# A fused transformer layer on one core: first modulation parts and first input chunks regrouped by K

## The chip, the cores and the metric

The kernel runs on one core of one Trainium2 chip. The metric is the device time of one execution in microseconds; lower is better. The times are medians of three runs.

## The reference

One encoder layer in float32 for a sequence of 256 rows and a width of 2048. A vector c gives shift, scale and gate (six vectors of 2048, `mod = silu(c) @ w_mod + b_mod`), and everything after it hangs on the first two of them:

```python
mod = silu(c) @ w_mod + b_mod                    # 2048 -> 6 * 2048
sh1, sc1, gt1, sh2, sc2, gt2 = split(mod, 6)
h = x * (1.0 + sc1) + sh1                        # (256, 2048)
proj = h @ w_in                                  # 2048 -> 5828 columns
p_a, p_b, p_c, p_d = split(proj, (A_COLS, B_COLS, C_COLS, D_COLS))
y = concat(rwkv7(p_a), sparse_attention(p_b), chunk_attention(p_c), retention(p_d))
x = layer_norm(ALPHA * x + (1 + gt1) * (y @ w_out))
h = x * (1.0 + sc2) + sh2
gate, up = split(h @ w_up, (D_FF, D_FF))
x = layer_norm(ALPHA * x + (1 + gt2) * ((silu(conv(gate)) * up) @ w_down))
```

The columns A of the input projection belong to RWKV: r, k and v of 512 columns each, and 256 "lora" columns. Group B holds the queries of the sparse attention and, among others, 256 indexer columns (QI).

## The kernel before

**The input pass.** The product with w_in runs over 12 blocks of output columns, each over 16 K tiles of 128 rows. Its unit is the chunk: two K tiles by 512 columns (512 KB), 96 chunks in all (`N0_OUT`, 8 a block, `CH_IN`). Float32 is made of two parts: ScalarE copies a chunk from RAW to WHI as fp32r (`split_hi`), VectorE writes the rest to WLO (`split_lo`), and TensorE sums three products a tile (`fm`, 24 matmuls a chunk). h is split in the same way, to HHI and HLO. RAW, WHI and WLO are rings of four chunks; SP issues the load of chunk n once the low part of chunk n - 4 is done, and splits run 3 chunks ahead of TensorE (`AHEAD`).

**The order of the chunks.** `chunk_at(n)` gives block and K pair. Blocks 0 (r) and 1 (k) are interleaved: chunks 0 to 3 and 4 to 7 are the first eight K tiles of blocks 0 and 1, chunks 8 to 15 the other eight. From chunk 16 on it is block after block: 2 is v, 3 is lora and QI together, 4 and 5 are B, 6 to 8 C, 9 to 11 D. Each block has two of the four PSUM banks G (`pair`).

**The modulation.** w_mod is read by POOL as tiles of 128 partitions by 1024 columns (512 KB, one row of 4 KB a partition) into the four buffers of MODR; 16 tiles make a part of 1024 columns, and 12 parts make the whole. VectorE adds each tile, times a column of silu(c), to ACC (`mod_add`, L781 for the first tile of a part, L784 for the others; `mod_done` counts them and frees the buffer). TensorE sums over the partitions (`mod_reduce`, 8 matmuls with one column), and VectorE adds the bias (`mod_cols`, L791). The first four parts are shift and scale, in the order `FIRST_PARTS`: first half of the shift, first half of the scale, then the second halves. After the first two, h for K tiles 0 to 7 can be made (`dve.tensor_scalar` at L829, ScalarE L505, `h_split` L816), and chunks 0 to 7 run (`FIRST_CHUNKS`); after the other two, h for K tiles 8 to 15.

**Order by hand.** Every engine has its instruction order written out. After the first chunks the engines walk through n and its two halves: in each they have a chunk half, a number of mod tiles (`mods_at`), and a step of other work: `SETUP` (RWKV's preparation: squares, norms, four reciprocals "inverse", lora, cumulate, hats), the RWKV stages (`RW`, 21 stages for each of 4 units, from chunk `RW_FROM` = 35 on), and from `AT_FROM` = 79 on the attention and retention steps (`MIX`). When a block is done (`DONE_IN`), ScalarE and VectorE evacuate it (`evac_in`); for RWKV's columns these are 14 tiles of PA (L513, L852). VectorE executes in order, so a wait in an evacuation also holds the next low part behind it.

## Time and profile before

| | us |
|---|---|
| median of 3 runs | 1523.93 (1523.52 to 1525.11) |
| profiled execution, span | 1521.2 |
| TensorE busy (PE) | 1358.8 |
| VectorE busy (DVE) | 1025.9 |
| ScalarE busy (ACT) | 558.0 |
| TensorE's waits for VectorE's ACC | 73.6 |

A row of the timeline has start and duration in us, engine, source line, operation, the tiles written and read with their shapes, the count, and in square brackets the idle time before it with what ended it. A line of the table by windows has the window, its length, busy time of each engine with its number of instructions, the granted clock of TensorE (1.00 is 2.4 GHz, 0.50 is 1.2 GHz), the mean busy share of the 16 DMA engines and GB/s. The line number L1347 is the helper of all matmuls, so the tiles tell them apart.

### The profile page before, as it was taken

How to read it: one execution, taken by the hardware profiler on the slowest of the kernel's cores; microseconds unless marked ns; L12 is line 12 of the kernel's file. 1: busy time of each engine (PE TensorE's matmuls, PEld its weight loads, DVE VectorE, ACT ScalarE, POOL GpSimd, SP SyncE). 2: the span in 40 equal slices, each digit the busy share in tenths (PEclk: the TensorE clock that was granted, in tenths of full speed). 3: DMA queues.
4: the chain of work that ended last, by engine and by line, in shares of the span. 5: the costliest groups of instructions: out<-in, count | busy, mean ns of one | idle time of the engine just before them, and what ended most of it. 6: DMA issues, size and time to landing. Idle time of an engine off the chain costs nothing.

```text
span 1521.2 us, 23831 instructions
## 1 busy us (share of the span) xinstructions
PE 1358.8 (89%) x9247; PEld 1252.2 (82%) x9247; DVE 1025.9 (67%) x1320; ACT 558.0 (37%) x771; POOL 137.3 (9%) x221
## 2 busy tenths in 40 slices
PE   1172998999999999998699999999999999999994
PEld 1172998998979667786699999999999998888883
DVE  4787778768787986566977877655556555545545
ACT  2021553213233342443344444444444444333331
POOL 2222010100000110100600000000000000000001
PEclk8585999889999998999899999999999999999997
DMA  9898884645555764665178786554655656766561
GB/s 354 314 338 309 268 276 130 200 144 180 194 167 167 277 233 141 246 226 178 55 280 288 251 289 196 162 181 147 199 183 175 193 179 193 244 199 193 181 205 57
DMA packets 142951, 319.08 MB, mean 210 GB/s; under 512 B 12238, under 2 KB 19744, under 8 KB 141856
## 3 DMA queue, kind: packets, MB, share of 16 engines
q1 hardware_dynamic: 114656, 213.23, 43.1%
q0 software_dynamic: 28224, 104.87, 20.2%
q8 instruction: 48, 0.79, 0.2%
q14 instruction: 23, 0.19, 0.0%
HBM read 315.97 MB, written 2.10 MB: 209 GB/s over the span
## 4 chain that ended last, share of the span: by engine, by line
PE 47%; DVE 2%; issue 1%; DMA 1%; ACT 0%; DVEq 0%; ACTq 0%; SPq 0%
PE G L1347 46%; DMA RAW<-in_w_up_dram 1%; PE M L1347 0%; DVE WLO L770 0%; DVE X L1331 0%; DVE X L1340 0%; DVE X L1338 0%; DVE SM L1259 0%; ACT WHI L487 0%; DVE ACC L1250 0%; DVE GF L1266 0%; DVE HLO L816 0%; DVE X L1314 0%; DVE SM L1316 0%; DVE SM L1255 0%
## 5 line engine op out<-in xcount | busy, mean ns | idle before, releaser
L1347 PE MATMUL G<-HHI,WHI 128*128 128x256 f32 x1952 | 566.1, 290 | 19.3 <-issue 7.2
L1347 PE MATMUL G<-HLO,WHI 128*128 128x256 f32 x1952 | 557.5, 286 | 0.0
L1347 PE MATMUL G<-HHI,WLO 128*128 128x256 f32 x1952 | 557.3, 286 | 0.0
L1347 PEld LDWEIGHTS G<-HHI,WHI 128*128 128x128 f32 x1952 | 379.8, 195 | 23.4 <-issue 20.0
L1347 PEld LDWEIGHTS G<-HLO,WHI 128*128 128x128 f32 x1952 | 380.1, 195 | 0.5 <-issue 0.5
L1347 PEld LDWEIGHTS G<-HHI,WLO 128*128 128x128 f32 x1952 | 379.8, 195 | 0.0
L765 DVE TENSOR_TENSOR WLO<-RAW,WHI 128x1024 fp32r<-128x1024 f32 x210 | 256.2, 1226 | 175.1 <-ACT WHI L481 172.9
L481 ACT ACTIVATE WHI<-RAW 128x1024 fp32r<-128x1024 f32 x210 | 221.5, 1060 | 316.0 <-PE G L1347 274.9
L770 DVE TENSOR_TENSOR WLO<-RAW,WHI 128x1024 fp32r<-128x1024 f32 x174 | 210.5, 1228 | 153.7 <-ACT WHI L487 153.7
L487 ACT ACTIVATE WHI<-RAW 128x1024 fp32r<-128x1024 f32 x174 | 179.8, 1054 | 202.0 <-PE G L1347 144.0
L784 DVE SCALAR_TENSOR_TENSOR ACC<-MODR,SM,ACC 128x1024 f32<-128x1024 f32 x150 | 191.8, 1279 | 30.4 <-DMA MODR<-in_w_mod_dram 27.9
L1347 PE MATMUL G<-WHI,FHI 128*128 128x512 f32 x352 | 136.9, 389 | 0.0
L1347 PE MATMUL G<-WLO,FHI 128*128 128x512 f32 x352 | 136.9, 389 | 0.0
L1347 PE MATMUL G<-WHI,FLO 128*128 128x512 f32 x352 | 136.9, 389 | 0.0
L1347 PE MATMUL G<-WHI,HHI 128*128 128x512 f32 (+1 forms) x256 | 102.8, 401 | 0.0
L1347 PE MATMUL G<-WHI,HLO 128*128 128x512 f32 (+1 forms) x256 | 99.8, 390 | 0.0
L1347 PE MATMUL G<-WLO,HHI 128*128 128x512 f32 (+1 forms) x256 | 99.4, 388 | 0.0
L1347 PE MATMUL M<-CFT,ACC 128*128 128x1 f32 x192 | 27.4, 274 | 73.8 <-DVE ACC L784 73.6
L1347 PEld LDWEIGHTS M<-CFT,ACC 128*128 128x128 f32 x192 | 27.1, 227 | 74.6 <-DVE ACC L784 74.0
L422 POOL DMA_DIRECT2D MODR<-in_w_mod_dram x96 | 50.8, 529 | 401.7 <-DVE ACC L784 367.0
L1347 PEld LDWEIGHTS G<-WHI,FLO 128*128 128x128 f32 x352 | 66.1, 188 | 13.8
L1347 PEld LDWEIGHTS G<-WLO,FHI 128*128 128x128 f32 x352 | 66.1, 188 | 13.8
(257 smaller groups left out, 1345.5 us busy)
## 6 DMA issues: line engine op xcount, KB each, us to landing
MODR<-in_w_mod_dram POOLq DMA_DIRECT2D x192, 512.0 KB, 5.0
RAW<-in_w_up_dram SPq DMA_DIRECT2D x176, 512.0 KB, 4.5
RAW<-in_w_down_dram SPq DMA_DIRECT2D x88, 512.0 KB, 4.3
RAW<-in_w_in_dram SPq DMA_DIRECT2D x80, 512.0 KB, 4.7
...
```

Of the source, the lines that this page charges most:

```text
L422: pool.dma_start(MODR[:, t % RING, :], wm[:, t, ds(m * MOD_W, MOD_W)])\
L481: act.activation(WHI[:, s, :, :], RAW[:, s, :, :], ACT.Copy).then_inc(hi_done, 1)
L487: act.activation(WHI[:, s, :, :], RAW[:, s, :, :], ACT.Copy).then_inc(hi_done, 1)
L765: dve.tensor_tensor(WLO[:, s, :, :], RAW[:, s, :, :], WHI[:, s, :, :].bitcast(f32), ALU.subtract).then_inc(lo_done, 1)
L770: dve.tensor_tensor(WLO[:, s, :, :], RAW[:, s, :, :], WHI[:, s, :, :].bitcast(f32), ALU.subtract).then_inc(lo_done, 1)
L784: ins = dve.scalar_tensor_tensor(a, w, ck, a, ALU.mult, ALU.add)
L1347: return pe.matmul(out_, l, r, start=start, stop=stop, skip_group_check=True)
```

## The change

The first four modulation parts become four groups. Group m reads shift and scale of the same 512 columns, so a tile of MODR has two rows of 2 KB for each partition, 2048 columns apart in w_mod. After group m, h for K tiles 4m to 4m + 3 is made. The input pass then sums all RWKV columns for these four K tiles: 7 chunks, two of k, one of lora (four K tiles by 256 columns, a view `wide` of the same ring slot), two of r and two of v. For that 7 PSUM banks are open at once: four G banks for k and r, M0 and M1 for v, M2 for lora. The norms step uses M3 and M2 in place of M0 and M1. Three groups (21 chunks) run before the last group of h is there, and 28 chunks finish RWKV's columns. QI follows as a block of four chunks of its own (four K tiles by 256 columns), and the rest is as before. The setup steps stand at chunks 23 to 31, RW_FROM is 33. VectorE takes two mod tiles beside each group's h in place of four beside each half. SP waits for the tenth mod tile before the first weight chunk.

```diff
-FIRST_PARTS = [0, 2, 1, 3]
-FIRST_CHUNKS = CH_IN
-MODS_BESIDE_H = 4
+GROUPS = 4
+GROUP_CHUNKS = 7
+FIRST_CHUNKS = (GROUPS - 1) * GROUP_CHUNKS
+MODS_BESIDE_H = 2
+K_BLOCK, R_BLOCK, V_BLOCK, QI_BLOCK, LORA = 0, 1, 2, 3, "lora"
 def chunk_at(n):
-    b, j = divmod(n, CH_IN)
-    q = CH_IN // 2
-    return (n // q % 2, n % q + n // CH_IN * q) if b < 2 else (b, j)
+    g, i = divmod(n, GROUP_CHUNKS)
+    if g < GROUPS:
+        b = [K_BLOCK, K_BLOCK, LORA, R_BLOCK, R_BLOCK, V_BLOCK, V_BLOCK][i]
+        return (b, 4 * g, 4) if b == LORA else (b, 4 * g + 2 * (i in (1, 4, 6)), 2)
+    if n < 4 * CH_IN:
+        return QI_BLOCK, 4 * (n - GROUPS * GROUP_CHUNKS), 4
+    b, j = divmod(n, CH_IN)
+    return b, 2 * j, 2
+DONE_IN = {23: K_BLOCK, 24: LORA, 26: R_BLOCK, 28: V_BLOCK, 32: QI_BLOCK} | \
+          {CH_IN * (b + 1): b for b in range(4, N_IN_BLOCKS)}
-SETUP = {(20, 0): "squares", (20, 1): "norms", (22, 0): "inverse 0", (24, 0): "inverse 1", (26, 0): "inverse 2",
-         (28, 0): "inverse 3", (32, 1): "lora", (33, 0): "cumulate", (34, 0): "hats"}
-RW_FROM = 35
+SETUP = {(23, 1): "squares", (24, 1): "norms", (25, 0): "inverse 0", (25, 1): "inverse 1", (26, 1): "inverse 2",
+         (27, 1): "inverse 3", (29, 1): "lora", (30, 1): "cumulate", (31, 1): "hats"}
+RW_FROM = 33
 def mods_at(n, half):
     if n < RW_FROM:
-        return int(half == 1 and n >= FIRST_CHUNKS + 6 and n % 3 != 1)
+        return int(n >= FIRST_CHUNKS and (half == 1 or n >= GROUPS * GROUP_CHUNKS))
...
-    return (2 if n == AT_FROM + 1 else 1) if AT_FROM <= n < N_IN_BLOCKS * CH_IN - 2 else 0
+    return (2 if (n, half) == (AT_FROM + 1, 0) else 1) if AT_FROM <= n < AT_FROM + 15 else 0
...
         def pair(b):
+            if b == V_BLOCK:
+                return M[0], M[1]
+            return (M[2],) if b == LORA else (G[2 * (b % 2)], G[2 * (b % 2) + 1])
...
             for n in range(N0_OUT):
-                b, j = chunk_at(n)
-                if n == CH_IN + RING:
+                b, kt, kts = chunk_at(n)
+                if n == 0:
+                    sp.wait_ge(mod_done, 10)
+                if n == FIRST_CHUNKS + 3:
                     sp.dma_start(CBT[:, :], const_b.bitcast(bf16)).then_inc(late_in, 16)
...
-                if n == 2 * CH_IN:
+                if n == FIRST_CHUNKS + 5:
                     sp.wait_ge(h_lo, KT)
...
-                pool.dma_start(MODR[:, t % RING, :], wm[:, t, part_at(m) * MOD_W:(part_at(m) + 1) * MOD_W])\
-                    .then_inc(mod_in[t % RING], 16)
+                pool.dma_start(MODR[:, t % RING, :].rearrange("p (s n) -> p s n", s=2),
+                               wm6[:, t, 0:2, m * 512:(m + 1) * 512]).then_inc(mod_in[t % RING], 16)
...
+            for g in range(GROUPS):
+                mod_add(g + 1, 0)
+                mod_cols(g)
+                dve.wait_ge(mod_col, g + 1)
+                for kt in (4 * g, 4 * g + 1):
+                    h_new_tile(kt)
+                for kt in (4 * g, 4 * g + 1):
+                    h_split(kt, 0)
+                for kt in (4 * g + 2, 4 * g + 3):
+                    h_new_tile(kt)
+                mod_add(g + 1, 1)
+                for kt in (4 * g + 2, 4 * g + 3):
+                    h_split(kt, 0)
+                if g == 0:
+                    for n in range(AHEAD):
+                        split_lo(n)
+                if g < GROUPS - 1:
+                    for t in range(MODS_BESIDE_H, KT):
+                        mod_add(g + 1, t)
+                        if t % 2:
+                            split_lo(g * GROUP_CHUNKS + t // 2 - 1 + AHEAD)
...
-            first_parts((0, 1))
             for n in range(N0_OUT):
-                if n == FIRST_CHUNKS:
-                    first_parts((2, 3))
+                if n <= FIRST_CHUNKS and n % GROUP_CHUNKS == 0:
+                    first_parts((n // GROUP_CHUNKS,))
```

## Rows read from the trace of the kernel before

**Rows 1.** The page, part 1: busy time, share of the span, instructions.
```profile
PE 1358.8 (89%) x9247; PEld 1252.2 (82%) x9247; DVE 1025.9 (67%) x1320; ACT 558.0 (37%) x771; POOL 137.3 (9%) x221
```

**Rows 2.** Table by windows: PE, PEld, DVE, ACT, POOL, clock, DMA share, GB/s.
```profile
0.00:41.30 41.30, 6.38 (x36) 6.18 (x37) 20.44 (x20) 9.39 (x16) 10.51 (x25) 0.87 0.94 352
41.30:70.60 29.30, 4.34 (x21) 4.26 (x21) 23.23 (x20) 0.00 (x0) 9.31 (x17) 0.50 0.88 300
70.60:105.20 34.60, 29.15 (x212) 28.49 (x211) 31.52 (x40) 10.65 (x16) 8.45 (x16) 0.84 0.93 336
105.20:139.20 34.00, 1.47 (x13) 1.38 (x12) 22.31 (x20) 0.85 (x1) 7.92 (x15) 0.55 0.98 357
139.20:235.30 96.10, 89.13 (x700) 87.92 (x699) 72.95 (x92) 50.09 (x75) 10.10 (x19) 0.95 0.75 248
```

**Rows 3.** Waits of TensorE, whole span: us in total, times, longest.
```profile
PE M L1347 <- DVE ACC L784: 73.6, 3, 32.5
```

**Rows 4.** Table by windows, two stretches with different traffic.
```profile
1000.00:1100.00 100.00, 100.00 (x815) 98.08 (x815) 54.19 (x65) 42.99 (x48) 0.00 (x0) 1.00 0.57 175
...
100.00:110.00 10.00, 5.80 (x49) 5.51 (x47) 7.80 (x9) 2.12 (x2) 2.38 (x5) 0.93 1.03 409
```

**Rows 5.** The page, part 3, DMA queues: packets, MB, share of 16 engines.
```profile
q1 hardware_dynamic: 114656, 213.23, 43.1%
q0 software_dynamic: 28224, 104.87, 20.2%
```

**Rows 6.** Timeline of VectorE, mod tiles and a low part, from 82 us.
```profile
82.29 2.66 DVE L784 SCALAR_TENSOR_TENSOR ACC<-MODR,SM,ACC 128x1024 f32<-128x1024 f32 x2
84.87 1.22 DVE L765 TENSOR_TENSOR WLO<-RAW,WHI 128x1024 fp32r<-128x1024 f32 x1
86.01 2.67 DVE L784 SCALAR_TENSOR_TENSOR ACC<-MODR,SM,ACC 128x1024 f32<-128x1024 f32 x2
```

**Rows 7.** Timeline of VectorE, the first half of h, from 70.6 us.
```profile
70.61 0.74 DVE L781 TENSOR_SCALAR ACC<-MODR,SM 128x1024 f32<-128x1024 f32 x1
...
73.43 0.73 DVE L829 TENSOR_SCALAR HTMP<-XT,MC 128x256 f32<-128x256 f32 x2
```

**Rows 8.** Timelines of VectorE and then TensorE around the restart at 146 us.
```profile
139.22 0.75 DVE L781 TENSOR_SCALAR ACC<-MODR,SM 128x1024 f32<-128x1024 f32 x1 [0.36 <-DMA MODR<-in_w_mod_dram]
...
146.08 0.55 PE L1347 MATMUL G<-HHI,WHI 128*128 128x256 f32 x1 [3.59 <-issue]
146.43 0.42 PE L1347 MATMUL G<-HLO,WHI 128*128 128x256 f32 x1
146.64 0.41 PE L1347 MATMUL G<-HHI,WLO 128*128 128x256 f32 x1
...
150.01 0.28 PE L1347 MATMUL G<-HLO,WHI 128*128 128x256 f32 x1
150.12 0.28 PE L1347 MATMUL G<-HHI,WLO 128*128 128x256 f32 x1
```

**Rows 9.** Groups by line of VectorE, 160 to 222 us: busy, mean ns.
```profile
L765 DVE TENSOR_TENSOR WLO<-RAW,WHI 128x1024 fp32r<-128x1024 f32 x21 | 25.4, 1215 | 3.3 <-ACT WHI L481 3.2
...
L873 DVE RECIPROCAL RN<-RN 128x256 f32<-128x256 f32 x4 | 7.0, 1745 | 0.0
L852 DVE SCALAR_TENSOR_TENSOR PA<-G,PCOL,PA 128x255 f32<-128x255 f32 x14 | 5.8, 476 | 5.1 <-ACT PA L513 5.1
```

**Rows 10.** Windows of TensorE alone: length, busy, clock, DMA share, GB/s.
```profile
230.00:235.00 5.00, 3.18 (x27) 1.00 0.11 25
...
290.00:295.00 5.00, 5.00 (x26) 0.50 0.89 300
```

**Rows 11.** Timeline of VectorE, cumulate, hats and the first gram stage.
```profile
229.06 0.74 DVE L888 TENSOR_TENSOR_SCAN CU<-SIG 128x128 f32<-128x128 f32 x2 [6.76 <-ACT AL L544]
...
234.92 0.48 DVE L905 SCALAR_TENSOR_TENSOR RK<-PA,PCOL,TA 128x256 f32<-128x256 f32 x1
...
242.03 0.75 DVE L929 TENSOR_TENSOR LT<-M,CBT 128x256 f32<-128x256 f32 x2
```

More of the change, by code:

```diff
@@ L302, in raw_count @@
         def raw_count(n):
-            double = sum(1 for m in range(n % RING, n + 1, RING) if m // CH_IN in (3, 5))
+            double = sum(1 for m in range(n % RING, n + 1, RING) if m // CH_IN == 5)
             return 16 * (n // RING + 1 + double)
@@ L500, in _ @@
             for kt in range(KT):
-                if kt == KT // 2:
-                    for n in range(FIRST_CHUNKS):
+                if kt and kt % 4 == 0:
+                    for n in range((kt // 4 - 1) * GROUP_CHUNKS, kt // 4 * GROUP_CHUNKS):
                         split_hi(n + AHEAD)
@@ L671, in _ @@
                     act.wait_ge(a_done, 1)
[L672 to L673 removed]
+                if n + 1 < N0_OUT and n + 1 in DONE_IN:
+                    evac_in(DONE_IN[n + 1])
             def y_tiles(rs):
@@ L805, in _ @@
             settle()
-            for t in range(KT):
-                mod_add(1, t)
-                if t == 3:
-                    mod_cols(0)
-                if t >= KT - AHEAD:
-                    split_lo(t - (KT - AHEAD))
             def h_split(kt, done):
@@ L845, in evac_in, with h_new_tile @@
-            def evac_in(b):
-                e, banks = evac[b % 2], pair(b)
-                if b <= 3:
-                    for i in range(4 if b < 3 else 2):
-                        j = 4 * b + i
-                        dve.wait_ge(mixed, 4 * b + 2 * (i // 2) + 2)
+            def h_new_tile(kt):
+                if kt >= 4:
+                    dve.wait_ge(h_lo, kt - 3)
+                dve.tensor_scalar(HTMP[:, kt % 4, :], XT[:, kt, :], MC[:, SC1 + kt:SC1 + kt + 1],
+                                  MC[:, SH1 + kt:SH1 + kt + 1], ALU.mult, ALU.add).then_inc(h_new, 1)
@@ L852, in evac_in @@
+            def evac_in(b):
+                e, banks = evac_lora if b == LORA else evac[b % 2], pair(b)
+                if b in A_TILES:
+                    for i in range(2 * len(banks)):
+                        j = A_TILES[b] + i
+                        dve.wait_ge(mixed, MIXED[b] + 2 * (i // 2) + 2)
                         dve.scalar_tensor_tensor(PA[:, j, 1:T], banks[i // 2][:, (i % 2) * T:(i % 2) * T + T - 1],
@@ L1154, in _ @@
                     gate_a()
-                if n + 1 in DONE_IN[:-1]:
-                    evac_in(DONE_IN.index(n + 1))
+                if n + 1 < N0_OUT and n + 1 in DONE_IN:
+                    evac_in(DONE_IN[n + 1])
             def two_parts(col):
@@ L1347, in mm, with fm @@
                 return pe.matmul(out_, l, r, start=start, stop=stop, skip_group_check=True)
-            def fm(s, kk, kt, banks, start, stop, tiles=4):
+            def fm(s, kk, kt, banks, start, stop, tiles=4, wide=lambda w, s: w[:, s, :, :]):
                 for i in range(tiles):
                     o = banks[i // 2][:, (i % 2) * T:(i % 2) * T + T]
-                    wh, wl = (w[:, s, kk, i * P:(i + 1) * P] for w in (WHI, WLO))
+                    wh, wl = (wide(w, s)[:, kk, i * P:(i + 1) * P] for w in (WHI, WLO))
                     mm(o, wh, HHI[:, kt, :], start=start and i % 2 == 0)
```

115 lines of the change are left out of this document (57 added, 58 removed).

## The prediction

> **What bounds the kernel now.** I read the page first. TensorE is busy 89% of a span of 1521.2 us, so only the places where it stands still, or runs at its half clock, can give time back [rows 1]. Then the table by stage [rows 2]: up to 139.2 us TensorE works 41 us (6.38, 4.34, 29.15 and 1.47), and the DMA share is 0.88 to 0.98. From 139.2 us on it is busy 89.13 of 96.10 us. The waits of TensorE name the reason [rows 3]: three waits on VectorE's ACC, 73.6 us in all. They are the waits for modulation parts (a part is 16 tiles of 0.524 MB). The input pass needs shift and scale of all 16 K tiles for each output block, and these are the first four parts. So the start is a stream of 64 mod tiles (33.5 MB), and TensorE has only 8 of the 96 chunks to do beside it. After it the pass is TensorE's: a chunk is 24 matmuls 0.12 us apart, 2.88 us [rows 8].
>
> How fast is the stream? Mod tiles alone take 29.3 us a part, 1.83 us each, at 300 GB/s and a DMA share of 0.88: that is four tiles in flight and not the DMA engines [rows 2]. With weight chunks beside them the same engines moved 409 GB/s at a share of 1.03 [rows 4].
>
> **Step 1, chunks under the stream.** After the change 21 chunks instead of 8 are done before the last part is in. The 13 moved chunks are 13 x 2.88 = 37.4 us of TensorE that no longer stand behind the stream. This is the gain, and the rest of the sum is what it costs.
>
> **Step 2, the stream gets longer.** I call T(k) the start of VectorE's step on mod tile k; before, T(16) is 41.3, T(32) 70.6, T(64) 139.2 us. T(16): the four first RAW loads (2.1 MB) wait for mod tile 10, so ten tiles come alone, then 6 tiles share with 4 chunks. I take 39 us (38 to 41.3). From T(16) to T(64) must then pass 48 mod tiles (25.2 MB), RAW chunks 4 to 25 (22, 11.5 MB) and the constants issued at chunk 24 (by their shapes 1.7 MB): 38.4 MB. At 409 GB/s these are 94 us, at the 336 GB/s of the stretch from 70.6 us 114 us [rows 2, 4].
> VectorE has a floor of its own: two mod tiles and one chunk's low part cost it 3.72 us (82.29 to 86.01) [rows 6], and a group has 7 of these, 26.0 us. The part beside h is mod tile 0, the wait for the column sums and mod_cols, 2.8 us (70.61 to 73.43), four h tiles of 0.33 + 0.33 us and mod tile 1 of 1.2 us [rows 7]: 6.8 us. That is 32.8 us a group, and 36.2 us for the first, which also splits chunks 0 to 2 (3 x 1.14). Three groups: 101.8 us. One group's bytes (23 tiles, 12.1 MB) in 32.8 us are 368 GB/s, so VectorE and DMA are about equally late and their jitter adds. I take 108 us (355 GB/s): T(64) = 147 us, 8 us later than before; bounds 141 and 164 (the latter at the 307 GB/s below).
>
> The first four parts are now read as two rows of 2 KB a partition instead of one of 4 KB. What shows of that: the POOL queue (4 KB rows) spent 20.2% of 16 x 1521.2 us on 28224 packets, 174 ns for 3.72 KB; the SP queue (2 KB rows mostly) 43.1% on 114656, 91.5 ns for 1.86 KB [rows 5]. That is 5% less per engine time, some 5 us on 33.5 MB, and it is inside my 355 GB/s. From the other side, a stretch with 2 KB rows alone had 175 GB/s at a share of 0.57, so 307 GB/s at full share [rows 4]; this gives 125 us and T(64) = 164 us. I stay near the mixed row, since the stream will be mixed. POOL's issue of a tile may grow from 0.53 us; at most one tile's worth, 0.5 us in a ring cycle of 7.3 us, and only where tiles come alone.
> The Trainium skill (Perfetto Trace Analysis, DMA Optimizations) speaks against this step: it says that going from 2 KB to 4 KB or 8 KB "can dramatically improve throughput", so halving rows would cost more than the 5% above. The rows of the two queues agree with the direction and not with the size; by its rule the 164 us end would be the likely one.
>
> Does TensorE keep up in the groups? It has 7 chunks, 20.2 us, in about 34 us. It ends each group early, waits for the next part, and starts again at 1.2 GHz, as at 76 and 146 us. Even with every chunk at half clock (0.21 us apart, 5.1 us) [rows 8] 35.8 us are needed against about 34 plus slack of three chunks, so I cost this at nothing; if the cover goes, about 1 us a group.
>
> **Step 3, the restart is shorter.** Before, from T(64) at 139.22 to TensorE's chunk at 146.08 are 6.9 us [rows 8]. After, two h tiles and not four-and-a-mod-tile stand ahead: 5.4 us. TensorE begins chunk 21 at 152.4 us; before it began chunk 8 at 146.1.
>
> **Step 4, the setup becomes VectorE's.** RWKV's preparation stood beside chunks 8 to 34, now it stands beside 21 to 32. The last of it (hats) let TensorE's turn go at 235.4 us. VectorE has between h and hats, with 0.09 us of each duration under the next: 11 splits of 1.14 (12.5), 15 mod tiles (7 x 1.19, 4 pairs of 2.58: 18.6), 14 PA updates of 0.39 (5.5), 4 reciprocals of 1.66 (6.6), 0.8 for the norms' maxima, 2.2 for cumulate (229.06 to 231.3) and 1.05 for hats [rows 9, 11]: 47.3 us. TensorE has 35 us of chunks there and 4 us of small steps, so it waits. VectorE is free 3 us after TensorE's start; with 2 us of in-order waits (PA updates wait for chunk 22's end and for ScalarE) hats ends 52 us after chunk 21 began: 204.4 us, 31 us before today's 235.4. What is queued behind each of these VectorE waits is the next chunk's low part, and TensorE waits for that; at chunks 28 to 32 two mod tiles a chunk want 423 GB/s, which the full rings (4 MB) cover; if not, 2 to 4 us.
> After hats stand two more mod tiles than today ahead of the gram products (today 235.3 to 242.0) [rows 11]: 2.3 us.
>
> **Step 5, the position.** RWKV begins at chunk 33, not 35, so two chunks more (5.8 us) stand behind this point. From there both kernels run the same stages beside the same number of chunks. The mod tiles are the same in number (96 after the first four parts; two of them moved from beside h to later). In block 5 (chunks 40 to 47, 68-column matmuls) TensorE ran 26 us at 1.2 GHz, 290 to 316 us [rows 10], beginning at stage rhs1 of unit 0. After the change rhs1 stands at chunk 42 and not 44, still in block 5, followed by the same stages; I leave it as it is. The end of the pass: two chunks without mix work, where y_tiles waits today about 2 us; at nothing, perhaps 2 us gained.
>
> **Sum:** 31.0 - 2.3 - 5.8 = 22.9 us, less 1 for reserve in the crossing at 28 to 32: 22 us. The profiled execution's 1521.2 us would be 1499 us; the median stands 2.7 us above its span, so 1523.9 - 22 = 1502 us.
>
> **The rivals.**
> A: 2 KB rows are slow. The stream runs at 307 to 331 GB/s; T(64) is 155 to 164 us and the gain 5 to 14 us: 1510 to 1519 us. For it: the 336 GB/s average of today's mixed stretch and the 307. Against: 409 at full queues.
> B: the half clock spreads, the case on the other side. In block 5 TensorE is near the point where its clock falls. If gram2 to turn, which now come at the block's first chunks, put the whole block at 1.2 GHz, its 8 chunks and stages last 88 us and not 44: 44 lost in place of today's 13, 31 us more, and the kernel ends at 1524 + 9 = 1533 us. It decides for slower from 22 us of extra loss, 44 us more at half clock. Against it: before, the chunks 40 to 43 ran at full clock beside dx stages, and at 230 to 235 us TensorE busy 3.18 of 5 us kept it [rows 10].
> The Trainium skill (TensorE: Matmul & The Clock Gate, Part 1) says that the default clock is the throttled one and activity releases it; TensorE waits a third of step 4 there, so by it some of step 4 might be at half clock too, which VectorE's pace would hide up to about 4 us a chunk against 5.1: 1.1 x 12 = 13 us at most.
> C: the same stage is missed by the half clock because the chunks meet it differently: 13 us more gain, 1489 us.
> D: the gain is given back in the attention stage or at the output projection, where VectorE is as late as TensorE: within 3 us of today. Against: these stages keep their mod tiles and stages per chunk, only shifted.
> E: the change does not do what it says (TensorE idles in the groups because low parts come after the next part's tiles): a gain under 10 us; it is in A's range.
>
> **How the numbers follow.** Forecast 0.62; A and E 0.18; B 0.07; C 0.08; D 0.05. The predicted time is the forecast's. Its own range is 1495 to 1509 us. For 8 in 10 I leave out B, D and the ends of A and C: 1489 to 1516 us. A difference under 0.2% (3 us) can't be told from none. Faster by more: 0.62 + 0.17 + 0.08 = 0.87; within: 0.05 (D) and 0.01 of A, 0.06; slower: 0.07.
>
> **What would show it.** TensorE starts a third time near 75 and a fourth near 112 us, the chunk after the last part near 152; VectorE without DMA waits over 10 us in 39 to 147 us (step 2); more than 20 us of TensorE idle between 152 and 210 us, ended by VectorE's WLO (step 4); RWKV's first turn near 204 us; after it all stages earlier by about 22 us, to the end. Wrong, if T(64) is over 155 us (A), if the granted clock is 0.5 for more than 35 us in block 5 (B), or if turn is early and the end is not (D).

## The result and the profile after

The changed kernel takes 1500.88 us (median; its runs span 1495.07 to 1511.2) against 1524.13 us before (1523.52 to 1525.11). The ratio is 0.9857, with a 95% interval of 0.9814 to 0.99: 1.4% faster, 1 us from the forecast of 1502 us. The profiled execution took 1511.2 us, the slow end of its spread; its span is 1509.4 us. The spread itself is part of the result: 16 us, and 1.6 us in the four runs of before beside it. Those four flatter it: 50 more executions of before, on four chips, lie between 1510.3 and 1533.6 us, all but three of them over 1519 us (the three: 1510.33, 1515.81 and 1517.63 us).

The page of the changed kernel, busy time and then the slices of the granted clock and the DMA engines:

```profile
PE 1371.2 (91%) x9247; PEld 1264.5 (84%) x9247; DVE 1026.0 (68%) x1320; ACT 557.7 (37%) x771; POOL 150.0 (10%) x221
...
PEclk8778789699999999898899999999999999999997
DMA  9999885555465774755278776565565565766561
```

It answers to [rows 1]: TensorE does the same 9247 matmuls; its busy time is 12 us longer, and the time around it is shorter. The table by stage, cut at T(16), T(32), T(48), T(64), the end of the hats and on to block 5; columns are length, busy time and count of PE, PEld, DVE, ACT and POOL, clock, DMA share, GB/s:

```profile
0.00:42.90 42.90, 7.29 (x38) 7.08 (x38) 20.48 (x21) 8.79 (x15) 14.56 (x26) 0.83 0.92 329
42.90:83.70 40.80, 26.38 (x188) 26.09 (x187) 33.87 (x35) 9.86 (x12) 12.00 (x17) 0.75 0.91 331
83.70:121.70 38.00, 26.58 (x186) 26.11 (x186) 30.21 (x34) 8.80 (x11) 11.58 (x16) 0.81 0.89 314
121.70:161.60 39.90, 26.58 (x188) 26.32 (x188) 30.32 (x34) 8.80 (x11) 10.87 (x16) 0.76 0.96 336
161.60:220.00 58.40, 49.82 (x338) 47.68 (x339) 51.73 (x69) 32.51 (x56) 9.03 (x17) 0.85 0.80 276
220.00:277.00 57.00, 53.01 (x432) 51.57 (x431) 48.19 (x83) 12.11 (x35) 7.43 (x14) 0.97 0.57 181
277.00:305.00 28.00, 28.00 (x143) 26.91 (x143) 15.15 (x32) 6.54 (x25) 3.19 (x6) 0.57 0.57 177
```

Beside [rows 2]: TensorE is now busy for 26.4 to 26.6 us in each of three groups (at a clock of 0.75 to 0.81), where it did 4.34 and 1.47 us in two of the stretches before. But a group lasts 38 to 41 us, not 34 to 36, and T(64) is 161.6 us, not 147. The waits of TensorE up to 245 us (us in total, times, longest):

```profile
PE M L1373 <- DVE ACC L806: 44.3, 4, 16.0
...
PE G L1373 <- DVE HLO L836: 6.1, 3, 2.0
PE G L1373 <- DVE WLO L787: 5.6, 1, 5.6
PE M L1373 <- DVE PA L878: 4.6, 2, 2.3
```

The 73.6 us of [rows 3] are 44.3 us now. The times used below, as a list (us; T(k) as in the prediction; "hats" is the start of the last RK step, "gram" the first LT step, "indexer" its first matmul on BK and BQI, "retention end" the first YD <- YD, DG, "second h" the first HTMP after the output projection). The experiments are in it too, since most of them are read by it:

| kernel | T(16) | T(64) | hats | gram | indexer | retention end | second h | span |
|---|---|---|---|---|---|---|---|---|
| before | 41.3 | 139.2 | 234.9 | 242.0 | 496.9 | 622.0 | 724.7 | 1521.2 |
| after | 42.9 | 161.6 | 219.0 | 228.8 | 484.7 | 608.4 | 715.0 | 1509.4 |
| again | 42.5 | 158.0 | 215.0 | 224.8 | 467.8 | 593.1 | 698.2 | 1492.6 |
| rows_only | 42.6 | 142.3 | 237.6 | 244.7 | 502.3 | 622.0 | 729.5 | 1523.8 |
| wide_rows | 40.7 | 152.9 | 209.4 | 220.0 | 479.7 | 604.1 | 710.9 | 1505.8 |
| two_groups | 42.5 | 148.5 | 222.7 | 232.4 | 488.3 | 613.6 | 716.8 | 1512.1 |
| no_sp_wait | 42.6 | 159.7 | 216.7 | 226.4 | 469.4 | 593.4 | 700.0 | 1494.4 |
| late_consts | 42.3 | 156.8 | 220.8 | 231.4 | 474.8 | 600.1 | 705.0 | 1502.6 |
| fewer_mods | 43.7 | 158.5 | 214.3 | 223.8 | 467.0 | 592.1 | 695.4 | 1490.6 |
| block5_early | 43.2 | 159.0 | 216.1 | 226.5 | 476.8 | 600.6 | 704.0 | 1499.3 |
| light_mods | 39.9 | 149.0 | 205.8 | 216.4 | 459.6 | 583.3 | 687.8 | 1483.1 |
| wide68 | 42.8 | 160.8 | 217.4 | 228.0 | 483.1 | 605.2 | 712.1 | 1507.8 |
| deep_ring | 37.0 | 148.2 | 203.6 | 214.2 | 470.4 | 595.7 | 700.7 | 1495.2 |
| best | 40.5 | 145.5 | 200.5 | 210.4 | 453.4 | 581.2 | 686.3 | 1481.9 |

### The profile page after: what moved, and what is told of

Same layout as the page of the kernel before. It is cut to its first block, busy times and chain, and to the rows that moved or that the text cites. A ratio compares the mean times of both kernels' runs of the same rounds, so it can differ in the third digit from the quotient of the medians.

```text
span 1509.4 us, 23866 instructions
## 1 busy us (share of the span) xinstructions
PE 1371.2 (91%) x9247; PEld 1264.5 (84%) x9247; DVE 1026.0 (68%) x1320; ACT 557.7 (37%) x771; POOL 150.0 (10%) x221
## 4 chain that ended last, share of the span: by engine, by line
PE 49%; DVE 2%; issue 0%; DVEq 0%
PE G L1373 49%; PE M L1373 0%; DVE X L1357 0%; DVE X L1366 0%; DVE X L1364 0%; DVE SM L1285 0%; DVE WLO L792 0%; DVE HLO L836 0%; DVE X L1340 0%; DVE SM L1342 0%; DVE ZT L1338 0%; DVE SM L1281 0%; DVE SM L1226 0%; DVE ACC L1276 0%; DVE SM L1361 0%
## 5 line engine op out<-in xcount | busy, mean ns | idle before, releaser
L1373 PE MATMUL G<-HHI,WHI 128*128 128x256 f32 x1856 | 543.3, 293 | 20.7 <-DVE WLO L787 9.1
L1373 PE MATMUL G<-HLO,WHI 128*128 128x256 f32 x1856 | 533.9, 288 | 0.0
L1373 PE MATMUL G<-HHI,WLO 128*128 128x256 f32 x1856 | 533.4, 287 | 0.0
L1373 PEld LDWEIGHTS G<-HHI,WHI 128*128 128x128 f32 x1856 | 365.6, 197 | 25.7 <-issue 18.8
L787 DVE TENSOR_TENSOR WLO<-RAW,WHI 128x1024 fp32r<-128x1024 f32 x210 | 256.4, 1227 | 167.9 <-ACT WHI L500 165.7
L1373 PEld LDWEIGHTS G<-HLO,WHI 128*128 128x128 f32 x1856 | 365.7, 197 | 0.6 <-issue 0.5
L1373 PEld LDWEIGHTS G<-HHI,WLO 128*128 128x128 f32 x1856 | 365.1, 197 | 0.0
L1373 PEld LDWEIGHTS G<-WHI,FHI 128*128 128x128 f32 x352 | 66.1, 188 | 13.8
L1373 PE MATMUL M<-CFT,ACC 128*128 128x1 f32 x192 | 31.3, 294 | 45.8 <-DVE ACC L806 44.3
```

The costliest lines, as they stand in the source:

```text
L787: dve.tensor_tensor(WLO[:, s, :, :], RAW[:, s, :, :], WHI[:, s, :, :].bitcast(f32), ALU.subtract).then_inc(lo_done, 1)
L1373: return pe.matmul(out_, l, r, start=start, stop=stop, skip_group_check=True)
```

## Experiments

The question that the result leaves: the time came out as forecast, but the stream ended 14.6 us later. So something else must have given these back. The runs ask what the stream costs, and why executions differ by 16 us. A ratio below is that to the kernel before, run beside it on the same chip, with its 95% interval. All stage times are those of one execution each. The six executions with the same stream (after, again, no_sp_wait, fewer_mods, block5_early, wide68) have T(64) at 158.0 to 161.6 us, mean 159.6, and 114.8 to 118.7 us from T(16) to T(64), mean 116.7: a difference of under 4 us against one of them is not clear of their spread.

**again**: the changed kernel, unedited.

> The changed kernel once more, unedited, to see another execution of it. Its times spread over 1495 to 1511 us where the kernel before stays within 1.6 us. If the spread comes from the stream of mod tiles, a faster execution than the first one (span 1509.4 us, last group's tile T(64) at 161.6 us) has T(64) earlier by about the difference of the spans, 147 to 155 us. If it comes from TensorE's clock, T(64) stays at 160 to 163 us and the half-clock stretches of the input pass (275 to 305 us in the first one) are shorter.

1504.06 us (1494.38, 1509.56, 1498.56, 1513.06), 0.9882 (0.9829 to 0.9935). Its profiled execution is at the fast end (1494.38 us). Against after's, of the 16.8 us between the two spans 3.6 lie at T(64), and 12.9 between gram and indexer (255.9 against 243.1 us): the second reading of the expectation, though T(64) at 158.0 us lies in neither of its ranges. (That before stays within 1.6 us, as the expectation has it, does not hold in the 19 executions beside this one: 1510.3 to 1533.6 us.) The same stretch of time is the last line of the table by stage in after, and in again:

```profile
275.00:305.00 30.00, 29.27 (x249) 28.63 (x248) 24.95 (x45) 7.17 (x21) 3.70 (x7) 1.00 0.71 220
```

TensorE is busy in both; at a clock of 0.57 it does 143 matmuls in 28 us, at 1.00 it does 249 in 30. It is one program: the half clock in block 5 comes in some executions and stays away in others.

What TensorE did before the fall is the same in both. First after: the wait, and TensorE alone from 278 us on; then again, at the same place of the program:

```profile
275.18 0.43 PE L1373 MATMUL M<-MST,AR 64*128 64x64 f32 x2 [0.76 <-DVE MST L1004]
278.00:283.00 5.00, 5.00 (x23) 0.50 0.90 295
```

```profile
271.18 0.43 PE L1373 MATMUL M<-MST,AR 64*128 64x64 f32 x2 [0.77 <-DVE MST L1004]
274.00:279.00 5.00, 5.00 (x42) 1.00 0.89 288
```

TensorE waits 0.8 us for VectorE's MST, a step of RWKV, in both; in after the clock is granted at half from 277.9 us on, in again it stays. The seven profiled executions that have the stretch in block 5 (before, rows_only, after, wide_rows, two_groups, wide68, deep_ring) have this wait of 0.73 to 0.76 us, and their clock falls 1.3 to 3.0 us after it; the six in which it stays away have the same wait at 0.75 to 0.77 us. So the wait goes ahead of every fall and doesn't decide it. No run takes it out.

**rows_only**: the kernel before, with the first four parts read as 2 KB rows of shift and scale. The order of chunks is the old one.

```
-    wm[:, t, part_at(m) * MOD_W:(part_at(m) + 1) * MOD_W]
+    wm6[:, t, 0:2, m * 512:(m + 1) * 512]
```

> The kernel before with one thing of the change: the first four modulation parts are read as shift and scale of the same 512 columns, two rows of 2 KB a partition, all else as before. My sum had 5% less rate on 33.5 MB, so T(64) 2 to 5 us later than 139.2 us and 1526 to 1529 us. The rival that 2 KB rows are slow (307 GB/s) has T(64) at 150 us or later and 1535 us or more. Below nothing: if the landing order of smaller rows helps, 1522 us.

1525.77 us, 1.0016 (0.9988 to 1.0045). T(16) to T(64) is 99.7 us instead of 97.9, and T(64) comes 3.1 us later. By this pair of executions 2 KB rows cost 2 to 3 us of the stream, as the sum had it and not the rival; in the end of the kernel they can't be told from nothing.

**wide_rows**: the changed kernel with 4 KB rows again. It leaves out that shift and scale of the same columns come together: h is made with other columns of w_mod. All transfers and instructions are there.

```
-    wm6[:, t, 0:2, m * 512:(m + 1) * 512]
+    wm[:, t, m * MOD_W:(m + 1) * MOD_W]
```

> The changed kernel with the first four parts read in rows of 4 KB, 1024 columns next to each other as before. It leaves out that shift and scale of the same columns come together, so h is made with other columns of w_mod; the bytes, instructions and order are the same. By my sum T(64) comes 3 to 6 us earlier than with 2 KB rows in the same run and the time is 1495 to 1498 us. By the rival of slow 2 KB rows T(64) falls from 161 to 147 us and the time by 12 us or more, to 1489 us.

1505.28 us (1507.66, 1493.48, 1505.23, 1505.33), 0.9844 (0.9795 to 0.9894): as again, and not the 1495 to 1498 us expected; its profiled execution has the half clock in block 5 (259.7 us from gram to indexer). T(16) to T(64) is 112.2 us against 115.5 in again and 118.7 in after. Its three groups:

```profile
40.65:80.20 39.55, 26.96 (x188) 26.67 (x188) 33.78 (x36) 9.85 (x12) 8.70 (x17) 0.76 0.94 347
80.20:115.10 34.90, 25.83 (x185) 25.57 (x185) 30.35 (x34) 8.80 (x11) 8.44 (x16) 0.79 0.94 344
115.10:152.90 37.80, 25.53 (x185) 25.27 (x186) 30.35 (x34) 8.79 (x11) 8.38 (x16) 0.77 0.95 343
```

So with 4 KB rows the stream still takes 4 us more than the 108 of the forecast, and the share is still 0.94: T(64) is 5.1 us earlier than in again, 0.9 of them from its beginning, where the forecast missed again's by 11. The rows are less than half of the error (5.1 of 11 us; 3.3 of it between T(16) and T(64), which is not clear of the spread); the rest is something else.

**two_groups**: only 14 chunks under the stream, the third group's 7 after it.

```
+    for n in range(2 * GROUP_CHUNKS, 3 * GROUP_CHUNKS):    # after the last part, on ScalarE and VectorE
+        split_hi(n + AHEAD)                                # split_lo likewise
...
-    if n <= FIRST_CHUNKS and n % GROUP_CHUNKS == 0: first_parts((n // GROUP_CHUNKS,))
+    if n in (0, 7): ...;  if n == 14: first_parts((2, 3))
```

> The changed kernel with only 14 chunks under the stream: the seven chunks of the third group are split and summed after the last part, with the fourth group's. By my sum the stream is shorter by their 3.7 MB, 8 to 11 us, and by up to 8 us of VectorE's steps in the third group; 20.2 us of TensorE's work and seven low parts come behind it: a loss of 8 to 14 us, 1509 to 1515 us. If the gain had come from elsewhere (the split of h into four, the spread of setup), the time stays within 3 us of the changed kernel's 1501 us.

1514.42 us, 0.9912 (0.9878 to 0.9946). T(64) comes 9.5 us before that of again, but from there to the hats it takes 74.2 us instead of 57.1. A chunk under the stream lengthens it by 9.5 / 7 = 1.4 us and takes 17.1 / 7 = 2.4 us from behind it. Steps 1 and 2 of the prediction are both there, at 2.4 us a chunk where step 1 had 2.88; and for these seven their balance is 1.1 us a chunk, not 2.3 (29.4 / 13 by the forecast's 37.4 and 8).

**no_sp_wait**: the wait of SP for mod tile 10 left out, so that the first four RAW loads start at once.

> The changed kernel without the wait of the first weight chunks for mod tile 10. By my sum the wait brought T(16) from 41.3 to 39 us; the trace shows 42.5 to 42.9 us with it. If the wait does nothing since the first 16 tiles and four chunks are the same bytes, T(16) is 41 to 43 us without it and the time the same within 2 us. If it costs, since the ring of four tiles can't fill the DMA engines alone between 16 and 26 us, T(16) is 1 to 2 us earlier without it.

1498.11 us, 0.9848 (0.9804 to 0.9892). T(16) is 42.6 as in again, T(64) 159.7: with four buffers the wait shows in neither.

**late_consts**: the constants (1.7 MB) three chunks later.

```
-    if n == FIRST_CHUNKS + 3:
+    if n == FIRST_CHUNKS + 6:
```

> The changed kernel with the constants and small weights of 1.7 MB loaded at chunk 27, after the last part of h, in place of chunk 24, inside the last group of the stream. If bytes set the length of the stream, T(64) comes 4 to 5 us earlier (1.7 MB at 370 GB/s) than 158 to 162 us, and the setup, which has DMA share to spare, is no longer: 4 us less in all, 1497 to 1500 us. If VectorE sets it, T(64) stays.

1512.66 us, 0.9917 (0.9885 to 0.995). The expectation was 1497 to 1500 us and T(64) 4 to 5 us earlier. T(64) is 1.2 us earlier than in again and 2.8 than the mean of the six, which leaves open how much the constants cost the stream; but from there to the hats it takes 64.0 us and not 57.1. Waits of ScalarE and of VectorE, 155 to 225 us:

```profile
ACT WHI L500 <- DMA RAW<-in_w_in_dram: 8.7, 2, 6.9
...
DVE WLO L787 <- ACT WHI L500: 7.0, 3, 5.9
```

The constants now stand ahead of a RAW load that the setup needs: the bytes have been moved to where they are waited for.

**fewer_mods**: the mod tiles beside chunks 28 to 31 one a chunk instead of two; the four others after RWKV.

```
-    return int(n >= FIRST_CHUNKS and (half == 1 or n >= GROUPS * GROUP_CHUNKS))
+    return int(n >= FIRST_CHUNKS and (half == 1 or n >= RW_FROM - 1))
-    ... if AT_FROM <= n < AT_FROM + 15 else 0
+    ... if AT_FROM <= n < AT_FROM + 17 else 0
```

> The changed kernel with four mod tiles fewer beside chunks 28 to 31 (one a chunk and not two) and four more beside chunks 92 and 93 after the mixing stages. If VectorE sets the length of the setup, T(64) to hats falls by 4 x 1.39 = 5.6 us from 57 us, and most of it reaches the end: 1496 to 1499 us. If the chain through TensorE and ScalarE (lora, tanh, sigmoid) sets it, hats stays within 1 us and the time too. At the end of the pass VectorE gets 5.6 us more beside chunks without mix work, which cost nothing unless the norm of retention waits for it.

1497.04 us, 0.9844 (0.9802 to 0.9885). T(64) to hats is 55.8 us instead of 57.1: 1.3 us gained for the 5 us of work that left. (The median lies in the range of the first theory by its executions: the profiled one has no stretch in block 5.) What VectorE then waits for, 158 to 216 us:

```profile
DVE WLO L787 <- ACT WHI L500: 4.5, 3, 3.3
DVE PA L878 <- ACT PA L533: 2.5, 2, 1.4
```

The setup is not VectorE's alone. Behind it stands the chain from TensorE's lora matmuls over ScalarE, which waits 6.7 us for them (its SIG) and has the next WHI behind that.

**block5_early**: the contents of blocks 4 and 5 exchanged, so that the 68-column matmuls come at chunks 32 to 39.

```
-    QI_BLOCK: [(bqi, 256)], 4: [(B0, GW)], 5: [(bkv, 128), (bqi + 256, 68)]
+    QI_BLOCK: [(bqi, 256)], 5: [(B0, GW)], 4: [(bkv, 128), (bqi + 256, 68)]
```

> The changed kernel with the contents of blocks 4 and 5 exchanged: the block with 68-column matmuls (keys, values and weights of the sparse attention) stands at chunks 32 to 39, beside turn, gram and the dx stages, and the full 512-column block of queries at 40 to 47, beside the small stages rhs0 to turn. One execution of the changed kernel had a stretch of 23 us at 1.2 GHz there and another had none, with 255.9 and 243.1 us from the first gram stage to the indexer. If the pair of 68-column matmuls and small stages lets the clock fall, the stretch is gone in every execution: 243 us, and a time of 1492 to 1497 us with a narrow spread. If it falls for a reason outside the kernel's work, stretches of 20 us and more still come in some executions, and the spread stays 15 us or more. If the 68-column block lets it fall by itself, the stretch moves to chunks 32 to 39 and the time stays or grows.

1499.11 us (1493.36 to 1501.25), 0.9833 (0.979 to 0.9877). TensorE alone at 220 to 244 us, and at the place where the stretch stood before; then late_consts, whose blocks are not exchanged:

```profile
220.00:244.00 24.00, 21.86 (x109) 0.57 0.55 182
277.00:305.00 28.00, 26.50 (x212) 1.00 0.69 225
```

```profile
220.00:234.00 14.00, 11.94 (x50) 0.51 0.98 347
```

This looks as if the half clock had moved with the columns, and it doesn't show it. TensorE waits 2.9 us for VectorE's AR at 219.3 us, and the clock falls there; other executions, late_consts above or wide_rows (0.53 from 215 to 226 us), have a half clock at this point of the program with the old blocks, for up to 13.6 us against 20.5 here. And that the stretch is missing at the old place happens to the unexchanged kernel too. For the block speaks that it lasts longer here, that gram to indexer is 250.3 us, between 243 and 255.9, and that none of the four is over 1501.25 us. That suggests the few columns as a cause to try; the next run takes them away.

**wide68**: block 5's 68-column matmuls stream 128 columns; the 60 more are not used.

```
-    o = banks[1][:, t * P:t * P + 68];   WHI[:, s, kk, 256:324], WLO[:, s, kk, 256:324]
+    o = banks[1][:, t * P:t * P + P];    WHI[:, s, kk, 256:384], WLO[:, s, kk, 256:384]
```

> The changed kernel, where the 68-column matmuls of block 5 stream 128 columns instead (the 60 more are not used). Theory 1, the half clock in block 5 is granted because those matmuls keep few columns of the array busy: no stretch at half clock between 277 and 320 us in the profile, the times bunch at 1493 to 1501 us and none is over 1503. Theory 2, it comes from the small RWKV stages or from something outside block 5: the stretch is there in some executions as before, times between 1494 and 1512 us. A matmul of 128 columns costs at most what one of 68 does plus 0.03 us, 96 of them: under 3 us.

1496.6 us (1509.74, 1497.34, 1494.92, 1507.34, 1495.87, 1495.12), 0.9833 (0.9801 to 0.9866). The stretch is still there in the profiled execution (TensorE alone):

```profile
278.00:300.00 22.00, 22.00 (x98) 0.50 0.64 205
```

Theory 1 falls: with 128 columns in these matmuls the clock falls as with 68. Two times near 1508 and four near 1496 show the same two groups of executions as before.

**light_mods**: VectorE adds 256 of the 1024 columns of tiles 1 to 15 of the first four parts (the rest of the sum is left out), so that its step costs about 0.5 us instead of 1.27.

```
+    if m < GROUPS:
+        a, w = a[:, 0:256], w[:, 0:256]
     ins = dve.scalar_tensor_tensor(a, w, ck, a, ALU.mult, ALU.add)
...
```

> The changed kernel, where VectorE adds only 256 of the 1024 columns of each tile 1 to 15 of the first four parts, so that its step costs about 0.4 instead of 1.2 us; the rest of the sum of shift and scale is left out. The transfers are all made. Some 36 us of VectorE's 102 us go out of T(16) to T(64). Theory 1, VectorE and the transfers are both needed in turns (full buffers, then the engines at their limit): that stretch shrinks from 115 to 119 us to 96 to 108 us. Theory 2, the transfers alone pace it: it stays within 3 us of 115. Theory 3, VectorE alone paces it: under 90 us. After T(64) nothing changes.

1488.66 us, 0.9769 (0.9738 to 0.98). T(16) to T(64) is 109.1 us, 6.4 less than again, for 34 us of VectorE work less (22.2, 18.8 and 18.7 us busy in the groups instead of 33.7, 30.2 and 30.3). Its groups:

```profile
39.90:79.90 40.00, 26.96 (x187) 26.68 (x187) 22.19 (x36) 9.72 (x12) 11.58 (x16) 0.76 0.94 341
79.90:112.60 32.70, 26.02 (x185) 25.76 (x185) 18.78 (x33) 8.79 (x11) 11.58 (x16) 0.81 0.98 358
112.60:149.00 36.40, 25.21 (x185) 24.96 (x186) 18.65 (x32) 8.79 (x11) 10.86 (x16) 0.83 1.01 366
```

It lies a microsecond above what theory 1 gave, 3 us below theory 2's range and far from theory 3's. With VectorE busy for 59.5 us and not 94, the transfers run at a share of 0.94 to 1.01 and still need 109 us: 354 GB/s is what the DMA engines gave here at full share. Of VectorE's 34 us only 6 had shown (8 against the mean of the six). From T(0) to T(64), which holds all of the bytes, it is 138.4 us here and 147.3 in again.

**deep_ring**: eight buffers instead of four for the first four parts. The four more lie at 154.25 KB, free until the setup.

```
+    MODX = sb("MODX", [P, RING, MOD_W], 154.25)
...
-    if q >= RING: pool.wait_ge(mod_done, q - RING + 1)
+    if q >= 2 * RING: pool.wait_ge(mod_done, q - 2 * RING + 1)
+    ring = MODR if t % 8 < RING else MODX
```

> The changed kernel with eight instead of four buffers for the tiles of the first four modulation parts (four more buffers lie in memory that is free until the setup); nothing else is changed. Theory 1, the stream stands still because its four buffers are full while VectorE makes h, and because four tiles in flight don't fill the DMA engines when they come alone: T(16) comes 3 to 7 us earlier (36 to 39.5 instead of 42.5 us), T(16) to T(64) shrinks from 115 to 119 us to 103 to 109 us, all of it reaches the end: 1480 to 1492 us. Theory 2, the stream is paced by the DMA engines at about 335 GB/s when 2 KB rows are in it: T(64) moves by under 3 us, 1496 to 1506 us. Theory 3, VectorE's own 101.8 us a stretch and its order are the pace: T(16) earlier, T(16) to T(64) not under 110 us.

1495.92 us (1483.26 to 1497.07), 0.9793 (0.9765 to 0.9821); theory 1 had 1480 to 1492 us. Five of the six are at 1494.8 to 1497.1 us, and the profiled one of them has the half clock in block 5. T(16) is 5.4 us earlier than in again, T(64) 9.7. First a group's beginning in again, then in deep_ring (windows of 10 us from T(16) on; the last two lines of again's are a part of its first):

```profile
42.45:52.45 10.00, 4.40 (x21) 4.32 (x22) 7.83 (x14) 3.48 (x6) 1.53 (x3) 0.50 0.69 241
52.45:62.45 10.00, 10.00 (x71) 10.00 (x71) 8.62 (x8) 2.42 (x3) 2.89 (x4) 0.81 0.98 337
46.45:48.45 2.00, 0.00 (x0) 0.00 (x0) 2.00 (x5) 1.17 (x4) 0.00 (x0) 0.50 0.47 184
48.45:50.45 2.00, 0.00 (x0) 0.00 (x0) 2.00 (x4) 0.63 (x1) 0.72 (x1) 0.50 0.01 2
```

```profile
37.00:47.00 10.00, 2.81 (x14) 2.73 (x13) 1.66 (x4) 2.38 (x4) 0.94 (x2) 0.50 1.04 381
47.00:57.00 10.00, 5.47 (x31) 5.47 (x32) 9.82 (x13) 2.63 (x6) 1.81 (x3) 0.57 0.86 286
```

With four buffers the transfers stand still while VectorE makes h (a share of 0.01 from 48.45 to 50.45 us, 0.69 over the ten), and afterwards VectorE waits for them while they run at their limit. With eight they go on. But T(16) to T(64) is 111.2 us, over theory 1's 109 and by its letter what theory 3 gave, and the second line shows a hole a step later. Its cause is on ScalarE, and VectorE's wait for it:

```profile
39.27 1.06 ACT L502 ACTIVATE WHI<-RAW 128x1024 fp32r<-128x1024 f32 x1 [2.86 <-DMA RAW<-in_w_in_dram]
45.68 1.06 ACT L502 ACTIVATE WHI<-RAW 128x1024 fp32r<-128x1024 f32 x1 [5.35 <-DMA RAW<-in_w_in_dram]
46.64 0.71 ACT L526 ACTIVATE HHI<-HTMP 128x256 fp32r<-128x256 f32 x2
```

```profile
DVE HLO L842 <- ACT HHI L526: 6.8, 4, 6.3
```

The splits of chunks 0 to 2 stand ahead of the first h copy in ScalarE's order. SP let their loads start only after mod tile 10, when eight mod tiles were queued. The wait that had cost nothing with four buffers costs 6.3 us here.

**best**: eight buffers, SP's wait left out, and fewer_mods' places of the mod tiles. It ran on another chip than deep_ring.

> The kernel with eight buffers for the first four parts, without the wait of the first RAW loads for mod tile 10, and with the mod tiles beside chunks 28 to 31 one a chunk (the 4 others after RWKV). In the run with eight buffers alone VectorE waited 6.3 us for ScalarE's first HHI copy, which stood behind the split of chunk 2, whose load had been queued behind eight mod tiles. Theory 1, that wait comes from the late start of the first RAW loads: here it is under 1.5 us, T(16) comes at 37 to 40 us, T(64) at 143 to 148 us (148.2 with eight buffers alone), the hats end 54 to 57 us later, and the time is 1478 to 1492 us. Theory 2, the transfers are at their limit all the way, so that their order doesn't matter: T(64) stays at 148 us or over, and the time is 1488 to 1497 us. The half clock in block 5 comes and goes as before and makes a spread of 13 us in either.

1482.71 us (1481.48 to 1484.41), 0.9729 (0.9707 to 0.9752): 2.7% faster than before, and 18 us faster than the change. Waits of VectorE, 20 to 160 us:

```profile
DVE MC L818 <- PE M L1377: 6.7, 4, 2.6
DVE ACC L810 <- DMA MODX<-in_w_mod_dram: 3.8, 7, 0.8
DVE ACC L810 <- DMA MODR<-in_w_mod_dram: 2.5, 4, 0.8
...
DVE HLO L840 <- ACT HHI L524: 0.5, 3, 0.2
```

Theory 1 holds: the wait on HHI is 0.5 us, T(64) is 145.5 us, the hats come 55.0 us later. T(16) is 40.5, half a microsecond over what it gave and later than deep_ring's 37.0, since the RAW loads now go first. T(0) to T(64) is 135.1 us, against 137.5 in deep_ring. The DMA engines are now the limit of the stream: from T(16) to T(64), first in after and then in best, all engines:

```profile
42.90:161.60 118.70, 79.53 (x559) 78.53 (x558) 94.40 (x100) 27.45 (x34) 34.45 (x49) 0.77 0.92 327
40.50:145.50 105.00, 79.91 (x564) 79.11 (x565) 93.96 (x99) 26.37 (x33) 31.96 (x45) 0.81 1.01 364
```

Of the 13.3 us between the spans of deep_ring and best, 3.8 are there at gram and 13.2 lie between gram and indexer (243.0 against 256.2 us), and best gives back 3.7 from there to the end: most of its lead over deep_ring is that the half clock in block 5 stayed away. The one execution of deep_ring at 1483.26 us is as fast as best's. None of best's five has the time of one with the stretch, where the expectation had a spread of 13 us; they ran on one chip, and neither the five nor the chip lets one say that it stays so.

## Why the prediction was right, and where it was not

**Step 1 (37.4 us).** Right in its mechanism. The three groups run under the stream, 26.5 us of TensorE each, and two_groups shows what undoing one of them does: 17.1 us behind the stream, where seven chunks at the forecast's price are 20.2.

**Step 2 (T(64) = 147 us, bounds 141 to 164).** This term was mis-sized: 161.6 us in the profiled execution; 158.0, 159.7, 158.5, 159.0 and 160.8 in again, no_sp_wait, fewer_mods, block5_early and wide68, which have the same stream. The bytes were right: 331, 314 and 336 GB/s over 40.8, 38.0 and 39.9 us are 38.8 MB, forecast 38.4. The rate was wrong. The forecast put 355 GB/s on the whole stretch, between VectorE's floor (102 us) and the engines' (94 us), and said that the two are about equally late. Two things were wrong in that. The floor of the engines was too low: the 409 GB/s of one window of 10 us [rows 4] were not held over any group. At full share the engines gave 354 GB/s in light_mods (0.98) and 364 in best (1.01), which is 105 to 108 us for 38.4 MB and not 94. So the 355 GB/s, meant to lie above both floors, were already all that the engines give, and nothing was left for the second: the two take turns. While VectorE makes h, the four buffers are full and nothing is fetched (a share of 0.01 for 2 us in again, 241 GB/s over 10 us); later the engines are full and VectorE waits, 17.2 us in after:

```profile
DVE ACC L806 <- DMA MODR<-in_w_mod_dram: 17.2, 15, 4.2
DVE MC L814 <- PE M L1373: 7.3, 4, 2.2
```

The 108 us from T(16) to T(64) were 118.7 in after and 115.5 in again. The runs give parts of it, and they overlap: 4 KB rows take 3.3 us from again's, eight buffers 4.3, eight buffers with the order mended 10.5. T(16) was 42.3 to 43.7 and not 39: the mod tiles that come alone are paced by four buffers, not by SP's wait (no_sp_wait 42.6, deep_ring 37.0). The wait for TensorE's column sums (MC, 7.3 us) was inside the forecast's 2.8 us for each h part. (The terms of that part, 2.8, 2.64 and 1.2 us, add up to 6.6 and not 6.8 us, half a microsecond in all.)

The Trainium skill (Perfetto Trace Analysis, DMA Optimizations) says that batching small transfers into larger ones, 2 KB into 4 KB or 8 KB for example, "can dramatically improve throughput". That does not decide here: rows_only shows 1.8 us in 98, about 2%, and wide_rows 3.3 us in 115, about 3%. Rival A came true at T(64) (161.6 us, in its 155 to 164) and in the profiled execution (1511.2 us, in its 1510 to 1519), but its cause did not: eight buffers moved T(64) by 9.7 us, 4 KB rows by 5.1.

The prediction's own sign says the same: "Wrong, if T(64) is over 155 us (A)". Of its other signs of the stream, there were to be no waits of VectorE for DMA over 10 us, and they are 17.2 us in all (the longest 4.2); and TensorE starts its next groups at 88.3 and 126.3 us, not near 75 and 112.

That TensorE keeps up in the groups at nothing was right: it ended each before the next part's sums and waited for ACC (44.3 us).

**Steps 3 and 4 (57.4 us from T(64) to the hats).** Measured 57.4 in after, 57.1 in again. The parts: TensorE restarted 4.1 us after T(64) (161.6 to 165.7), forecast 5.4; the hats 53.3 us later, forecast 52. VectorE was busy 51.7 us of the 58.4 and waited for TensorE, ScalarE or DMA for most of the rest. The groups of VectorE in that stretch, as they answer to [rows 9]:

```profile
L806 DVE SCALAR_TENSOR_TENSOR ACC<-MODR,SM,ACC 128x1024 f32<-128x1024 f32 x16 | 20.3, 1268 | 1.2 <-DMA MODR<-in_w_mod_dram 1.0
L787 DVE TENSOR_TENSOR WLO<-RAW,WHI 128x1024 fp32r<-128x1024 f32 x11 | 13.4, 1220 | 1.0 <-ACT WHI L500 1.0
L899 DVE RECIPROCAL RN<-RN 128x256 f32<-128x256 f32 x4 | 7.0, 1750 | 0.0
```

What was not right is the picture of TensorE: over 20 us of idle time were announced as the sign, and there are 8.6 us (49.82 busy of 58.4; 4.6 of them waits for PA, 2.0 for HLO, none for WLO), since it ran at a mean clock of 0.85 and was nearly as late as VectorE. That is the half clock under VectorE's cover that rival B's second part described, bounded there at 13 us; the cover held. The Trainium skill (TensorE: Matmul & The Clock Gate, Part 1) has the half clock as what TensorE falls to without activity. The trace agrees here, where TensorE had waited (11.3 us before 160.1 us, and 0.50 from 152 to 168 us). It is no guide to block 5, where TensorE was busy 28.00 of 28.00 us at 0.57 and had waited 0.76 us before the fall, as it had in again, where the clock stayed; no run shows what brings that one.

The two mod tiles ahead of gram: hats to gram is 9.8 us against 7.1 [rows 11], 2.7 instead of the 2.3 of the sum.

**Step 5 (5.8 us for two chunks, block 5 left as it is).** The chunks cost less. From gram to the second h it is 482.7 us before, 486.3 after and 473.4 in again; again's lies 12.9 lower for block 5, so both say 3.6 us. From indexer to the second h it is 227.8 us before, 227.2 in rows_only, which has before's order of chunks, and 230.3 in both after and again: 2.5 to 3.1 us for the two chunks. A part of the reason shows: TensorE's mean clock over that way is 0.94 before, 0.95 in rows_only and 0.96 in after and again. The longest stretch at half clock that before has there is in the stage of retention. TensorE alone, before at 595 to 605 us; then all engines of after in the same part of that stage:

```profile
595.00:600.00 5.00, 5.00 (x15) 0.50 0.35 105
600.00:605.00 5.00, 5.00 (x19) 0.50 0.00 0
```

```profile
549.50:613.00 63.50, 62.42 (x334) 48.82 (x334) 49.30 (x65) 29.20 (x51) 7.54 (x12) 1.00 0.50 159
```

That stretch alone doesn't account for it: rows_only is without it, reaches the retention end in 119.7 us from indexer where before takes 125.1, and then needs 107.5 us to the second h where before takes 102.7. From the second h to the end after and again are 2.1 us shorter than before; but so is rows_only (794.3 us), so the change has no part in these 2 us. The 2 us that the prediction guessed for y_tiles would stand before the second h and were not measured.

Block 5 in the profiled execution is as forecast: 255.9 us from gram to indexer against 254.8 before. Rival C (the stage is missed by the half clock, 13 us) is no other case than the forecast, but a second kind of execution of the same kernel: 243.0 to 243.4 us in again, no_sp_wait, fewer_mods, late_consts, light_mods and best, 255.1 to 259.7 in after, wide_rows, two_groups, wide68 and deep_ring, 12.9 us between again and after. The prediction gave it a chance of 0.08 as though it were all or nothing. Before and rows_only have the stretch in their profiles (254.8 and 257.6 us), and nearly all of before's 54 times lie where one has to be with it, so it seems rarer since the change; the few low times of before have no profile.

**The sum.** For the profiled execution: 22 us forecast, less 14.6 for the stream and 0.4 for gram, plus 2.2 for the two chunks and 3 for the last part (2, which rows_only has too) and the reserve (1), is 12.2; the spans differ by 11.8. For again: 22 less 11 for the stream, plus 5 for the same small terms, plus 12.9 for block 5, is 28.9; the spans differ by 28.6. The median of 1500.88 lies between the two kinds. So the forecast of 1502 us held by luck: two things that it had wrong stand against each other, a stream 11 to 15 us longer, and a half clock that stays away in about half of the executions (of the eight of after and again, four are at 1494 to 1499 us, three at 1509 to 1513, one at 1503; two have a profile). The step that was mis-sized is step 2: 108 us forecast, 118.7 and 115.5 measured.

**What stays open.** Why the clock falls in block 5 in one execution and not in the next. wide68 has the stretch with 128 columns in place of 68, so few columns are not what it needs. That the block brings it is not shown: block5_early has one profile, in which the clock falls at a wait of 2.9 us. Left are TensorE's wait for MST, VectorE's splits of that block (four steps a chunk) and SP's shorter rows, and none was tried alone. The chip is not ruled out either: the runs are on several, and best, without the time of the stretch in any of its five, is the only one on its chip.

## What to carry to other kernels

Two resources that are about equally late don't cost the larger of their floors when few buffers lie between them: add the time that the producer stands still while the consumer does something else, and take the producer's rate from a whole stage at full share and not from its best window (409 GB/s there, 354 to 364 held). Here four more buffers of 0.5 MB moved the end of the stream by 10 us, about as much as leaving out a third of the consumer's work (9 us), and by 2.7 more once the other queue's first loads no longer stood behind them. Work put under a stream that is near its limit lengthens it (1.4 us for each chunk, whose bytes come along, against 2.4 us saved), and when a kernel's times fall into two groups, a profile of each is wanted before either is explained.

## What the runs showed of the chip

A stretch of one program, with TensorE busy all of it, ran at a granted clock of 0.50 to 0.57 in some executions and at 1.00 in others: 12.9 us of 1500. The seven falls in block 5 came 1.3 to 3.0 us after the same wait of TensorE of 0.73 to 0.76 us, and that wait was there too where the clock stayed (0.77 us in again). The medians of four to six runs that hold both kinds move by several us with their mix: 1500.88 and 1504.06 us for one program.

128 instead of 68 columns in the matmuls of that block left the stretch where it was (0.50 from 278 to 300 us in wide68).

GpSimd's issue of a 0.5 MB tile takes 0.72 us with two rows a partition and 0.53 us with one (16 issues in a part: 11.58 us in after, 8.44 in wide_rows).

Four tiles of 0.5 MB in flight gave 300 GB/s [rows 2] where they came alone. In the first part eight gave 384 with the first weight chunks among them, where four gave 351 (again, 10 to 42.45 us):

```profile
10.00:37.00 27.00, 6.72 (x39) 6.51 (x39) 20.27 (x19) 6.02 (x12) 11.37 (x16) 0.90 1.03 384
```
